# First tiles of index and feed-forward on the un-normalised residual, with the row scale applied behind PSUM

## What is computed

```python
for l in range(DEPTH):
    h = h + hybrid_mixer(rms_norm(h, norm_mix[l]), ...)
    h = h + swiglu(rms_norm(h, norm_ffn[l]), w_gate_up[l], w_down[l])
return rms_norm(h, norm_final)
```

## Time and profile before

| | before |
|---|---|
| runs | 2662.81, 2663.05, 2668.85 us, median 2663.05 |
| profiled execution | span 2665.5 us from the first to the last instruction (its own time isn't listed) |
| PE busy | 2479.5 us (93%), 12250 products |
| PE weight loads busy | 2027.8 us (76%) |
| DVE, ACT, POOL busy | 1241.8, 1052.9, 1081.4 us |
| mean granted clock of TensorE | 0.969 |

### The profile page before, as it was taken

The page is one execution under the profiler, slowest core; times in us unless marked ns, Lnnn a source line. Parts: engine busy times, 40 slices in busy tenths (PEclk is TensorE's granted clock), DMA queues, the critical chain, the costliest instruction groups (busy, mean ns, idle before and its releaser), DMA issues.

```text
span 2665.5 us, 37493 instructions
## 1 busy us (share of the span) xinstructions
PE 2479.5 (93%) x12250; PEld 2027.8 (76%) x12250; DVE 1241.8 (47%) x2139; ACT 1052.9 (39%) x1718; POOL 1081.4 (41%) x533
## 2 busy tenths in 40 slices
PE   7989989999999999999988989889999999999997
PEld 5677877877778878888766878778777787788886
DVE  4676676544453333330147776765444532333302
ACT  6444444344442233331264444443444422333312
POOL 3263453423334444444342543634333344444443
PEclk9999999999999999999989999999999999999998
DMA  3111011012212222222221011110121222222222
GB/s 132 64 35 45 31 39 40 25 63 64 71 67 95 93 77 94 94 94 95 87 72 56 33 40 40 39 40 25 63 70 63 79 95 94 73 94 94 95 94 102
DMA packets 50909, 184.39 MB, mean 69 GB/s; under 512 B 5648, under 2 KB 5776, under 8 KB 50704
## 3 DMA queue, kind: packets, MB, share of 16 engines
q1 hardware_dynamic: 50832, 183.40, 20.3%
HBM read 181.28 MB, written 2.10 MB: 69 GB/s over the span
## 4 chain that ended last, share of the span: by engine, by line
issue 73%; POOL 25%; POOLq 1%; PE 0%; DVE 0%; ACT 0%; DVEq 0%
POOL w_lo L404 17%; POOL mt_even L432 3%; POOL mt_odd L432 2%; POOL qk_t L454 1%; POOLq L408 1%; POOL q_d L444 1%; POOL xn_lo L467 1%; POOL decay_s L437 1%; POOL k_bg L458 1%; PE bank L1222 0%; POOLq L403 0%; DVE normalised L802 0%; DVE residual L799 0%; DVE squares L799 0%; ACT squares L506 0%
## 5 line engine op out<-in xcount | busy, mean ns | idle before, releaser
L404 POOL TENSOR_TENSOR w_lo<-w_raw,w_hi 128x1024 fp32r<-128x1024 f32 x337 | 818.3, 2428 | 1486.2 <-ACT w_hi L493 1486.2
L1222 PE MATMUL bank<-xn_hi,w_hi 128*128 128x512 f32 x1936 | 792.3, 409 | 21.2 <-ACT z_raw L503 7.3
L1222 PE MATMUL bank<-xn_lo,w_hi 128*128 128x512 f32 x1936 | 791.0, 409 | 2.8 <-POOL xn_lo L467 1.8
L1222 PE MATMUL bank<-xn_hi,w_lo 128*128 128x512 f32 x1936 | 791.1, 409 | 0.0
L493 ACT ACTIVATE w_hi<-w_raw 128x1024 fp32r<-128x1024 f32 x337 | 356.3, 1058 | 661.4 <-PE bank L1222 658.5
L1222 PEld LDWEIGHTS bank<-xn_hi,w_hi 128*128 128x128 f32 x1936 | 373.0, 193 | 114.4 <-issue 21.9
L1222 PEld LDWEIGHTS bank<-xn_lo,w_hi 128*128 128x128 f32 x1936 | 373.1, 193 | 81.8 <-POOL xn_lo L467 5.9
L1222 PEld LDWEIGHTS bank<-xn_hi,w_lo 128*128 128x128 f32 x1936 | 373.6, 193 | 75.0 <-issue 6.3
L802 DVE SCALAR_TENSOR_TENSOR conv_acc<-x_raw,hconv,conv_acc 128x512 f32<-128x512 f32 x144 | 158.6, 1101 | 26.3 <-ACT conv_acc L503 23.1
L799 DVE TENSOR_TENSOR residual<-residual,bank 128x512 f32<-128x512 f32 x32 | 22.0, 686 | 293.4 <-PE bank L1222 293.2
L1222 PE MATMUL bank<-mid_hi,w_hi 128*128 (+1 forms) x352 | 139.4, 396 | 0.2
(11 more groups left out here) (235 smaller groups left out, 3677.5 us busy)
## 6 DMA issues: line engine op xcount, KB each, us to landing
w_raw<-w_tiles SPq DMA_DIRECT2D x338, 512.0 KB, 3.2
residual<-x_t SPq DMA_DIRECT2D x4, 512.0 KB, 5.6
out_t<-normalised SPq DMA_DIRECT2D x8, 256.0 KB, 2.2
rope<-rope SPq DMA_DIRECT2D x1, 1024.0 KB, 11.3
mats<-mats SPq DMA_DIRECT2D x1, 768.0 KB, 8.1
vecs_all<-vecs SPq DMA_DIRECT2D x1, 133.0 KB, 7.9
```

The costliest lines, as they stand in the source:

```text
L404: nc.gpsimd.tensor_tensor(w_lo[j][:], w_raw[j][:], w_hi[j][:].bitcast(F32), ALU.subtract).then_inc(s_lo, 1)
L1222: return nc.tensor.matmul(out, lhsT, rhs, start=start, stop=stop)
```

## The change

The first tiles behind a norm multiply rows that aren't normalised: `h` times the gain, split to a high and a low part by ACT (behind each square) and DVE (`raw_lo`). For the index these are all 5 tiles, for the feed-forward the first 4. The row scale is applied when the products leave PSUM: in the index through scaled rope tables `cos_r`, `sin_r` (and one DVE product for the head weights), in the feed-forward by DVE products with the scale. The sums of squares are now two wide fp32 products with a matrix of ones, which gives the sum on every partition, in the midst of the first tiles' products; root and reciprocal work on 128x512, and the diagonal and its broadcast are gone. The index's first two tiles do their products with high rows first (`hi_first`). The normalised rows for all later tiles are made while the first tiles run. The padding tile moves from the end of a layer to behind the third front tile (index 8 of the layer); it is still transferred and split. The first transfers come in another order. The first pass of the feed-forward loop is written out.

In the diff `...` marks what is left out.

```diff
         def _(sp):
+            sp.dma_start(vecs_all[:], vecs_in).then_inc(s_vecs, 16)
+            sp.dma_start(w_raw[0][:], w_tiles[0]).then_inc(landed[0], 16)
             for k in range(0, KD, 2):
                 sp.dma_start(h[:, k:k + 2, :], x_t[:, k:k + 2, :]).then_inc(s_x[k // 2], 16)
-            for dst, src in ((mats, mats_in), (vecs_all, vecs_in)):
-                sp.dma_start(dst[:], src).then_inc(s_in, 16)
-            for j in range(AHEAD):
-                sp.dma_start(w_raw[j][:], w_tiles[j]).then_inc(landed[j], 16)
+            sp.dma_start(w_raw[1][:], w_tiles[1]).then_inc(landed[1], 16)
+            sp.dma_start(mats[:], mats_in).then_inc(s_in, 16)
             sp.dma_start(rope[:], rope_in).then_inc(s_rope, 16)
...
-            def xn_lo_of(turn):
+            def xn_lo_of(turn, norm):
                 for k in POOL_LO:
                     pool.wait_ge(rms_a.sem, rms_a.after(turn, f"hi{k}"))
...
-            w_lo_of(0, 0)
+                    nc.gpsimd.tensor_tensor(xn_lo[:, k, :], norm[:, k, :], xn_hi[:, k, :].bitcast(F32), ALU.subtract).then_inc(rms_g.step(f"lo{k}"), 1)
+            for j in range(AHEAD):
+                w_lo_of(j, j)
             with pool.Fori(0, DEPTH) as l:
-                w_lo_of(l * TILES + 1, 1)
-                xn_lo_of(2 * l)
-                plain(l, 0, T0_GDN + 8)
+                plain(l, 0, 1)
+                xn_lo_of(2 * l, mix_norm)
+                plain(l, 1, T0_GDN + 8 - 1)
...
-                plain(l, T0_DSA + 4, T0_UP - T0_DSA - 4 - AHEAD)
-                for j in range(AHEAD):
-                    w_lo_of(l * TILES + T0_UP + j, (T0_UP + j) % 2)
-                xn_lo_of(2 * l + 1)
-                plain(l, T0_UP, TILES - T_PAD - T0_UP)
+                plain(l, T0_DSA + 4, T0_UP + 1 - T0_DSA - 4)
+                xn_lo_of(2 * l + 1, ffn_norm)
+                plain(l, T0_UP + 1, TILES - T0_UP - 1)
...
-            def square(k):
+            def square(k, squares, raw_hi, gain):
                 nc.scalar.activation(squares[:, k, :], h[:, k, :], ACT.Square).then_inc(rms_a.step(f"sq{k}"), 1)
...
+                copy(raw_hi[:, k, :], h[:, k, :], scale=gain[:, k:k + 1]).then_inc(rms_a.step(f"xh{k}"), 1)
+            def rms_root(turn, root, total):
+                act.wait_ge(rms_p.sem, rms_p.after(turn, "ss"))
+                nc.scalar.activation(root[:], total[:], ACT.Sqrt, bias=vecs_all[:, V_EPS:V_EPS + 1], scale=1.0 / D).then_inc(rms_a.step("sqrt"), 1)
...
@@ -529,6 +550,10 @@
                         act.wait_ge(idx_v.sem, idx_v.after(l, f"r{j - 2}"))
                     copy(ix0[j % 2][:], dense[j % 2][:]).then_inc(idx_a.step(f"x{j}"), 1)
                     swap(ixs[j % 2], dense[j % 2], IHD // 2, P if j < 4 else IHD).then_inc(idx_a.step(f"xs{j}"), 1)
+                    if j == 0:
+                        rms_root(2 * l, mix_root, bank[3])
+                    if j in (1, 2):
+                        rms_hi(2 * l, mix_norm, range(4 * j - 4, 4 * j))
...
                     if u == len(IR) // 2:
-                        tile_done(l, T0_GDN + 2)
-                        next_hi(l, T0_GDN + 2, (T0_GDN + 2) % 2)
+                        last = front_tile(0, BEFORE_PAD - 1)
+                        tile_done(l, last + T_PAD)
+                        for n in (last, last + T_PAD):
+                            next_hi(l, n, n % 2)
...
+            act.wait_ge(s_vecs, 16)
+            w_hi_of(0, 0, first=True)
             for k in ks:
                 act.wait_ge(s_x[k // 2], 16)
-                square(k)
...
+                square(k, mix_squares, mix_raw_hi, vecs_all)
+            w_hi_of(1, 1, first=True)
...
-                    square(m)
-                rms_root(l * 2 + 1)
+                    square(m, ffn_squares, ffn_raw_hi, vec[:, V_FFN:V_FFN + KD])
                 next_hi(l, T0_UP - 1, (T0_UP - 1) % 2)
-                rms_hi(l * 2 + 1)
-                with act.Fori(0, KF // 2) as i:
+                rms_root(l * 2 + 1, ffn_root, bank[5])
+                for half in range(2):
+                    next_hi(l, T0_UP + half, (T0_UP + half) % 2)
+                    rms_hi(l * 2 + 1, ffn_norm, range(4 * half, 4 * half + 4))
+                t = l * (KF // 2)
+                for j in range(2):
+                    act.wait_ge(up0_v.sem, up0_v.after(l, f"g{j}"))
...
                     act.wait_ge(dn_v.sem, dn_v.after(l, f"h{m}"))
-                    square(m)
-                    if m == 4:
-                        tile_done(l, last - 1)
+                    square(m, mix_squares, mix_raw_hi, next_gain)
+                    if m == 2:
                         next_hi(l, last - 1, (last - 1) % 2)
...
+            def raw_lo(turn, k, hi, lo, gain):
+                dve.wait_ge(rms_a.sem, rms_a.after(turn, f"xh{k}"))
+                stt(lo[:, k, :], h[:, k, :], gain[:, k:k + 1], hi[:, k, :].bitcast(F32), ALU.mult, ALU.subtract).then_inc(rms_v.step(f"xl{k}"), 1)
...
+            def rms_inverse(turn, root, out):
                 dve.wait_ge(rms_a.sem, rms_a.after(turn, "sqrt"))
-                V.reciprocal(rms_col[:, 2, :], rms_col[:, 1, :]).then_inc(rms_v.step("rstd"), 1)
-                dve.wait_ge(rms_v.sem, rms_v.after(turn, "rstd"))
-                tt_(chunks(rms_diag), ident.unsqueeze(1).to_broadcast([P, NC, P]),
-                    over_free(rms_col[:, 2, :]), ALU.mult).then_inc(rms_v.step("diag"), 1)
-                dve.wait_ge(rms_p.sem, rms_p.after(turn, "bc"))
-            def rms(turn, gain0):
-                stats(turn)
-                for k in ks:
-                    stt(sq[:, k, :], h[:, k, :], vec[:, gain0 + k:gain0 + k + 1], bank[3][:], ALU.mult, ALU.mult).then_inc(rms_v.step(f"y{k}"), 1)
+                V.reciprocal(out[:], root[:]).then_inc(rms_v.step("rinv"), 1)
+                dve.wait_ge(rms_v.sem, rms_v.after(turn, "rinv"))
...
+            def normalise(turn, gain0, norm, scale, those):
+                for k in those:
+                    stt(norm[:, k, :], h[:, k, :], vec[:, gain0 + k:gain0 + k + 1], scale[:], ALU.mult, ALU.mult).then_inc(rms_v.step(f"y{k}"), 1)
...
             def index(l):
+                rms_inverse(2 * l, mix_root, bank[3])
+                for dst, src, name in ((cos_r, cos_i, "cos_r"), (sin_r, sin_i, "sin_r")):
+                    tt_(dst[:], src, bank[3][:], ALU.mult).then_inc(idx_v.step(name), 1)
+                dve.wait_ge(idx_v.sem, idx_v.after(l, "sin_r"))
...
+                    if j == 4:
+                        tt_(ix0[0][IHD:, :], ix0[0][IHD:, :], bank[3][IHD:, :], ALU.mult).then_inc(idx_v.step("xr"), 1)
+                    rotary(idx_v, l, out, ix0[j % 2], ixs[j % 2], cos_r, sin_r, (f"c{j}", f"s{j}", f"r{j}"), P if j < 4 else IHD)
+                    if j < 2:
+                        normalise(2 * l, V_MIX, mix_norm, bank[3], range(4 * j, 4 * j + 4))
...
+                        sum_squares(2 * l + 1, m - 1, ffn_squares)
+                    if m >= 1:
+                        raw_lo(2 * l + 1, m - 1, ffn_raw_hi, ffn_raw_lo, vec[:, V_FFN:V_FFN + KD])
+                raw_lo(2 * l + 1, KD - 1, ffn_raw_hi, ffn_raw_lo, vec[:, V_FFN:V_FFN + KD])
+                rms_inverse(2 * l + 1, ffn_root, bank[5])
+                V.reciprocal(ffn_rinv[:], ffn_root[:]).then_inc(up0_v.step("rinv"), 1)
...
+                for j in range(2):
+                    dve.wait_ge(s_tile, l * TILES + T0_UP + 2 * j + 1)
+                    dve.wait_ge(up0_v.sem, up0_v.after(l, "rinv"))
+                    tt_(f_gate[j][:], bank[2 * j][:], ffn_rinv[:], ALU.mult).then_inc(up0_v.step(f"g{j}"), 1)
+                    if j == 0:
+                        normalise(2 * l + 1, V_FFN, ffn_norm, bank[5], ks)
...
+                    stt(f_mid[j][:], f_gate[j][:], 0.5, bank[2 * j + 1][:], ALU.mult, ALU.mult).then_inc(up0_v.step(f"m{j}"), 1)
+                    dve.wait_ge(up0_v.sem, up0_v.after(l, f"m{j}"))
+                    tt_(f_mid[j][:], f_mid[j][:], ffn_rinv[:], ALU.mult).then_inc(ffn_v.step(f"mid{j}"), 1)
...
+            def stats(turn, squares, total):
+                pe.wait_ge(rms_v.sem, rms_v.after(turn, f"sum{KD - 2}"))
+                pe.wait_ge(rms_a.sem, rms_a.after(turn, f"sq{KD - 1}"))
+                mm(total[:], ones, squares[:, 0, :], True, False)
+                mm(total[:], ones, squares[:, KD - 1, :], False, True).then_inc(rms_p.step("ss"), 1)
...
+                        raw_ready(2 * l, k, low)
+                of_index = Dense(l, 0, 0, T_IDX, bank_free, x=lambda m: (mix_raw_hi, mix_raw_lo), x_ready=x_ready, hi_first=True)
+                of_index.issue(4 * KD)
+                stats(2 * l, mix_squares, bank[3])
+                of_index.finish()
+                pe.wait_ge(idx_v.sem, idx_v.after(l, "xr"))
...
+                def up_first():
+                    def bank_free(m):
...
+                    d = Dense(l, T0_UP, T0_UP, 4, bank_free, x=lambda m: (ffn_raw_hi, ffn_raw_lo), x_ready=x_ready, banks=bank[:4])
+                    d.issue(2 * KD)
```

(4 more changed lines are left out.)

200 lines of the change are left out of this document (114 added, 86 removed).

## The result

The changed kernel takes 2693.95 us (median of 4 runs, 2692.64 to 2695.29) against 2663.20 us before: a ratio of 1.0108, 95% interval 1.0094 to 1.0123, 30.8 us slower. I had forecast 2714.0. In later comparisons the kernel before had medians of 2664.05 to 2666.35 us, so the loss is 28 to 31 us.

The account below looks back on a forecast made before the run. PE was taken as the bound, working only on statistics for 8.4 us at each norm. Start 20.9, feed-forwards 1.4, boundary 23.3 and end 5.3 sum to 50.9 us over 2663.05: 2714.0 us, range 2690 to 2728.

Parts of the forecast that it names:

- My own case: Whole kernel: reciprocal 3.8 to 4.5 us, clock term 1.3 to 3, small terms 2 to 7; 2703 to 2724, 72%.
- rival (b): At the norms the wide reciprocal costs like a one-pass operation, seven times 3.3 us less: 2691 us, 9%.
- Feed-forward norms: Ahead of each feed-forward, PE idles 8.2 us for the fourth tile's low weights and the clock falls: +0.7 us each.
- the clock: Behind PE's idle at feed-forward and index stages, products run slower: 2.7 us lost each time.
- Start: First norm: later transfers and late low weights delay tile 3 by 14.2 us; with small terms +20.9 us.
- the extra wait ahead of the transposes: Index stage, start and boundary: transposes of w wait for a DVE scaling behind the swaps, 1.5 us.
- Boundary: Norm between layers: tile 3 starts 16.6 us later, PE idles 19; with clock and small terms +23.3 us.
- End: Last norm: later last square, cold sums, root and reciprocal delay the first output row by 5.3 us.
- Wide reciprocal: At the norms, DVE's reciprocal over 128x512: 4.0 us, extrapolated from smaller ones with rising cost per element.
- The order on POOL is what decides: POOL makes normalised low parts before the fourth tile's low weights; PE idles 8.2 us at feed-forwards, 19 at the boundary's index.
- rival (a): Not slower: fourth tile's low weights never late, chain shorter by 8.2 us at a feed-forward, 19 at the index; 2648, 7%.
- (c): New DVE work collides with POOL, peeled-loop jumps stall engines, padding splits cost 5 each: some 20 us more, 2733, 8%.

Follow-up runs that it names:

- experiment 2: Shifted large-buffer start addresses: kernel before by 32 bytes, 2657.60 us; changed kernel, 2695.72; kernel before with early Tanh and 128-byte multiples, 2645.52, or 128 over 256, 2640.00.
- hybrid2: Kernel before with early Tanh, operands 128 over multiples of 256 bytes, raw rows for first four up-projection tiles, and VectorE, ScalarE, GpSimd reordered: 2618.61 us.
- wide_before: Kernel before with only wide sums, root and reciprocal in place of narrow sums, diagonal and broadcast; normalisation stays in front: 2667.80 us.

## Why the prediction was right or wrong

Sign and place were right: PE starved four times, and 2693.95 is within 2690 to 2728. The size was 20 us too large. My own case, 2703 to 2724 with 72%, missed; the time lies in the range because its lower end came from rival (b), whose cause was wrong, and that is luck.

- **Feed-forward norms** (+0.7 each; my terms add up to 978.85, which is +0.6): -1.5 and -0.1. The wait was 7.26 for 8.2, because two reciprocals took 6.7 us and not 8; the clock took 1.5 and 3.0 for 2.7.
- **Start** (+20.9): +19.3. Tile 0's end at 28.2 and the fourth tile's start (56.10 for 56.3) were right; the clock took 1.6 for 2.7 (the fourth tile 7.06 us against 5.45), the padding tile 1.5 for 2.5, the extra wait ahead of the transposes 1.9 for 1.5.
- **Boundary** (+23.3): 18.8 by these two traces, 20 to 21.6 against the other kernels. From the end of tile 0 to the fourth tile I had 28.1; measured 27.9. PE's idle in it was 16.5 for 19, since the third tile ended 11.3 us behind tile 0 and not 9: it had waited 2.33 us for ScalarE's copies (the line at 1362.81), and its first eight products came at 0.43 us, the pace of the half clock. Tile 0 ended 22.3 us after the last down product and not 23.8, the extra wait ahead of the transposes (1.9 for 1.5) was made up before the first score, if one counts by this trace of before, and the padding tile cost 1.5 for 2.5.
- **End** (+5.3): +4.6, by the reciprocal.
- **What I had at nothing**: two loops, -8.8; output projections and merges, 3.0 a layer by the runs of experiment 2 (1.3 of it the output projection), so -6.1. These 14.9 us are the larger part of the 20 by which I was off. The row of +0.4 in the table hides the merge's share in layer 0 behind 2 us of the stretch that varies by itself. The diff shows both causes: a first turn peeled off the loop, and a changed list of buffers. The 24 short waits for low weights stood in the waits of before, and the loads on ScalarE's timeline of the loop; I took neither as something that the change moves.
- **Wide reciprocal** (4.0, 3.8 to 4.5): 3.36, below my range. From 32 elements in 353 ns to 512 in 3360 is 6.3 ns an element; the rise of the slope from 5.6 to 7.1 that I carried on does not go on. (My "about 4.3" was a slip besides: a slope of 7.1 + 0.75 gives 4.1.) By 8.33 ns an element, the estimate from the Trainium skill (VectorE: DVE Perf Modes), it would have been 4.3 us; the measurement decides.
- **The cause.** "The order on POOL is what decides" named the right wait and nearly its length (7.26 for 8.2, 16.5 for 19), and from that I took rival (a)'s worth: 8.2 us at a feed-forward, 19 at the index, if the order were mended. The runs give 3.0 us for two feed-forward norms with only the weights moved and 6.6 for two index stages. The rival's point (the chain shorter than the tiles in front of it) was not reached by that reorder: behind the tile that waited stood the next tile that would. It was reached at the feed-forward, by hybrid2, only when VectorE, ScalarE and GpSimd were all reordered. At the index no run reached it. There the change moves the normalisation from a stretch in which VectorE and ScalarE had little else to do into one in which they copy, swap and rotate: in each index tile of before ScalarE is idle for 1.3 to 1.5 us and VectorE for 3.2 to 3.4. That its length then binds is shown for 5.8 us a stage; that a better order couldn't hide it is not shown.
- **Rivals**: (b), 2691, comes nearest in number and was wrong in cause: the reciprocal costs 3.36, not 0.69. For (c) I find collisions (VectorE's low part of 2.96 us beside a weight split, in every second output-projection tile), off the path: VectorE still waits 1.27 us for PE behind it. One of 2.86 us ahead of the last residual rows at the boundary is on it; that one I had counted.

## What to carry to other kernels

A wait's length is not what its removal brings: ask which work stands behind the one that waited, and test it by a reorder before believing the sum. Work moved off one path lands on another; it pays only where the engines that take it are idle in the new place. And read a diff for what it moves without saying so: the function table with which a loop is entered, and the start address of every buffer allocated behind a changed one.

## What the runs showed of the hardware

- The interval of a 128x512 product moved with where the moving operand starts: 0.2267 us at 128 over a multiple of 256 bytes, 0.2289 to 0.2333 at 0, 64, 96, 160 and 192 over it, in the stages of the table. In the kernel before this and the table load were worth 26 us together (2666.35 to 2640.00), nearly as much as the change cost.
- The feed-forward loop, entered with another table than its Tanh needs, loaded the table in every turn (22 times 1.28 us); a tiny activation ahead of the loop took 20 of the 22 away, and 0.50 us off each turn.
- The wide reciprocal (128x512 fp32) takes 3.35 to 3.36 us, from SBUF into SBUF or into PSUM alike (7 in after, 5 in wide_before).
- The same idle of 7.26 us was followed by a loss of 1.5 us in one layer and 3.0 in the other (granted clock 0.63 and then 1.00, against 0.50 and then 0.73).
